# A two-layer encoder trunk in fp32 on one core: the weight sums of the MLP's second product move from VectorE to adding transfers, two products change places, and the first chunk's orders of VectorE and ScalarE are rewritten

## The reference

```python
def sqrelu_mlp(h, w_up, w_down):
    return jnp.square(jax.nn.relu(h @ w_up)) @ w_down
...
h = rmsnorm(x, g_ffn_pre[i])
x = x + rmsnorm(sqrelu_mlp(h, mlp_w_up[i], mlp_w_down[i]), g_ffn_post[i])
```

## Time and profile before

| | us |
|---|---|
| median of three runs | 1180.52 |
| the profiled execution, its own time | 1182.78 |
| its span | 1180.8 |
| TensorE busy with matmuls | 1130.0 (96% of the span) |
| VectorE busy | 946.8 (80%) |
| ScalarE busy | 766.8 (65%) |
| mean granted TensorE clock | 0.985 of full speed |

### The profile page before, as it was taken

How to read it: one execution, slowest core, us unless ns; L and a number is a source line. 1 busy time by engine, 2 the same in 40 slices (tenths; PEclk the granted TensorE clock), 3 DMA queues, 4 the chain that set the end, 5 groups by cost and what they waited for, 6 DMA issues and landing times.

```text
span 1180.8 us, 18252 instructions
## 1 busy us (share of the span) xinstructions
PE 1130.0 (96%) x6462; PEld 984.0 (83%) x6462; DVE 946.8 (80%) x1356; ACT 766.8 (65%) x1266; POOL 280.5 (24%) x261
## 2 busy tenths in 40 slices
PE   8999999997999999999999999999988999999997
PEld 7788789885897997988887888879866997988976
DVE  5899965779788688788789888875779787787787
ACT  6778867555674483674787777765547573663763
POOL 5688850302002002001421111100301011011013
PEclk9999999998999999999999999999999999999999
DMA  5322133326749549465213332223619458466653
GB/s 164 101 63 71 36 110 100 142 81 121 193 117 195 143 125 214 102 184 108 55 54 89 77 84 62 80 81 90 232 54 186 135 147 193 121 147 161 159 153 98
DMA packets 135092, 142.54 MB, mean 121 GB/s; under 512 B 5821, under 2 KB 108221, under 8 KB 134506
## 3 DMA queue, kind: packets, MB, share of 16 engines
q1 hardware_dynamic: 112300, 109.68, 29.6%
q0 software_dynamic: 22640, 31.72, 17.1%
q10 hardware_dynamic: 78, 0.16, 0.0%
HBM read 132.90 MB, written 6.29 MB: 118 GB/s over the span
## 4 chain that ended last, share of the span: by engine, by line
PE 75%; DVE 15%; issue 5%; ACT 4%; DVEq 0%; DMA 0%; POOL 0%; ACTq 0%
PE psum L860 7%; PE psum L862 7%; PE psum L861 7%; PE psum L1190 6%; PE psum L1192 6%; PE psum L1191 6%; PE psum L1178 6%; PE psum L1177 6%; PE psum L1176 6%; DVE mraw L2501 2%; DVE wlo L2157 2%; PE psum L867 2%; PE psum L869 2%; PE psum L868 2%; PE psum L1402 2%
## 5 line engine op out<-in xcount | busy, mean ns | idle before, releaser
L1495 ACT ACTIVATE whi<-mraw 128x1024 fp32r<-128x1024 f32 x212 | 223.3, 1056 | 216.6 <-PE psum L1192 85.1
L2157 DVE TENSOR_TENSOR wlo<-mraw,whi 128x1024 fp32r<-128x1024 f32 x212 | 258.5, 1223 | 101.1 <-ACT whi L1495 100.9
L1190 PE MATMUL psum<-whi,aop_hi 128*128 128x512 f32 x448 | 182.4, 407 | 29.5 <-DVE wlo L2157 14.5
L1192 PE MATMUL psum<-whi,aop_lo 128*128 128x512 f32 x448 | 179.4, 400 | 0.0
L1191 PE MATMUL psum<-wlo,aop_hi 128*128 128x512 f32 x448 | 179.2, 400 | 0.0
L860 PE MATMUL psum<-hhi,whi 128*128 128x512 f32 x376 | 150.8, 401 | 0.8 <-DVE wlo L2146 0.5
L862 PE MATMUL psum<-hhi,wlo 128*128 128x512 f32 x376 | 146.9, 391 | 0.0
L861 PE MATMUL psum<-hlo,whi 128*128 128x512 f32 x376 | 146.8, 390 | 0.0
L1190 PEld LDWEIGHTS psum<-whi,aop_hi 128*128 128x128 f32 x448 | 87.1, 195 | 56.4 <-DVE acc L2619 14.4
L1178 PE MATMUL psum<-hhi,wlo 128*128 128x256 f32 x384 | 108.7, 283 | 0.0
L1177 PE MATMUL psum<-xlo,whi 128*128 128x256 f32 x384 | 108.7, 283 | 0.0
(11 more groups left out here) (314 smaller groups left out, 2780.3 us busy)
## 6 DMA issues: line engine op xcount, KB each, us to landing
mraw<-in_mlp_w_up SPq DMA_DIRECT2D x64, 512.0 KB, 5.2
mraw<-in_mlp_w_down SPq DMA_DIRECT2D x64, 512.0 KB, 4.6
mraw<-in_mlp_w_down POOLq DMA_DIRECT2D x32, 512.0 KB, 6.1
mraw<-in_mlp_w_up POOLq DMA_DIRECT2D x24, 512.0 KB, 6.0
wraw<-in_conv_pw_w SPq DMA_DIRECT2D x20, 512.0 KB, 4.5
wraw<-in_attn_w_in SPq DMA_DIRECT2D x16, 512.0 KB, 4.9
x_copy<-xT SPq DMA_DIRECT2D x2, 2048.0 KB, 6.4
xT<-x_copy SPq DMA_DIRECT2D x2, 2048.0 KB, 9.4
```

Source lines behind the costliest of these rows:

```text
L1190: pe.matmul(o, ah, wh, start=kt == 0 and (not kept or c == 0), stop=False)
L1192: return pe.matmul(o, al, wh, start=False, stop=kt == 3 and (not kept or c == CHUNKS - 1))
L1495: a.activation(split_unit(whi, e), raw_unit(l, c, e_), ACT.Copy).then_inc(s["m_hi"], 1)
L2157: d.tensor_tensor(split_unit(wlo, e), raw_unit(l, c, e_), split_unit(whi, e).bitcast(F32), ALU.subtract).then_inc(s["m_ready"], 1)
```

## The change

1. P5's additions (both halves, all chunks) and P6's (chunks 0 to 2) leave VectorE. `add_down` now issues them as adding transfers from HBM into B11's slot, for P5, P6 and P4 alike, each when the split of the product before it in the slot is ready. VectorE keeps P6's in the last chunk, on the loaded B22.
2. In chunks 0 to 2 TensorE's order becomes P1, P2, P5, P3, P6, P7, P4; the last chunk keeps the old one. Unit numbers go by `DOWN_AT`.
3. P7's adding transfer no longer waits for P5's sum. `block_sums` has a new order: up's P4 and down's P7 alternate by half, then P5's two, then down's P6 and the next up's P7 alternating, then P4's two.
4. The next chunk's up block B11 is loaded after unit 6 of down (P3's in the new order), where it was after unit 8. The x copy is issued ahead of the first chunk's down loads.
5. In the first chunk, unit 7's split moves: on ScalarE from behind `s_hi` of pair 0 to behind the fifth square, on VectorE from behind the fourth `relu` to behind two `h_whole`. Splits 8 to 11, `h_whole`, `s7` and the others are put in another order around it, and the two P5 additions there go.

```diff
+DOWN_ORDER = ((P1, P2, P5, P3, P6, P7, P4),) * 3 + ((P1, P2, P5, P6, P3, P7, P4),)
+DOWN_AT = tuple({i: 2 * n for n, i in enumerate(o)} for o in DOWN_ORDER)
...
@@ sync, mlp_loads
+                sp.wait_ge(s["x_done"], (KB, 3 * KB)[l])
+                sp.dma_start(x_copy, flat(xT[:, :, :])).then_inc(x_kept, 16)
                 for j, b in enumerate((B11, B21, B12, B22)):
                     for h in range(2):
                         down_half(0, b, h, 2 * j + 2)
-                    if j == 1:
-                        sp.wait_ge(s["x_done"], (KB, 3 * KB)[l])
-                        sp.dma_start(x_copy, flat(xT[:, :, :])).then_inc(x_kept, 16)
...
-                    for b, at_ in ((B12, 3), (B11, 9), (B21, 11), (B22, 13)):
+                    for b, at_ in ((B12, 3), (B11, 7), (B21, 11), (B22, 13)):
@@ gpsimd, add_down
                     pool.wait_ge(*loaded(r[B12], h, 2 * (CHUNKS * l + c) + 2))
-                    pool.wait_ge(s["t_sum"], t_nth(l, c, "down", h))
...
-                    pool.wait_ge(s["m_ready"], MLP_UNITS * l + DOWN[c] + 2 * P6 + h + 1)
-                    g.dma_start(raw_half(r[B11], h, D // 2), down_block(l, c, B21, h),
+                    last_use = {P5: P1, P6: P5, P4: P6}[i]
+                    pool.wait_ge(s["m_ready"], MLP_UNITS * l + DOWN[c] + DOWN_AT[c][last_use] + h + 1)
+                    g.dma_start(raw_half(r[B11], h, D // 2), down_block(l, c, PLUS[i], h),
                                 accum_op=ALU.add).then_inc(v4_sum[h], 16)
@@ gpsimd, block_sums
-                    for i in (P7, P4):
-                        for h in range(2):
-                            add_down(l, c, i, h)
-                        for h in range(2 if c < CHUNKS - 1 else 0):
-                            add_up(l, c + 1, i, h)
+                    for h in range(2):
+                        if c:
+                            add_up(l, c, P4, h)
+                        add_down(l, c, P7, h)
+                    for h in range(2):
+                        add_down(l, c, P5, h)
+                    for h in range(2 if c < CHUNKS - 1 else 0):
+                        add_down(l, c, P6, h)
+                        add_up(l, c + 1, P7, h)
+                    for h in range(2):
+                        add_down(l, c, P4, h)
@@ scalar, first chunk (the whole list of up)
                 for i in range(4):
                     up_square(g, 2 * i)
+                    if i == 2:
+                        m_hi(l, 7)
                     if i < 3:
                         up_square(g, 2 * i + 1)
                     else:
-                        m_hi(l, 10)
+                        m_hi(l, 8)
+                        m_hi(l, 9)
                     a1_hi(g, i)
                     if i == 3:
+                        m_hi(l, 10)
                         up_square(g, 7)
                     a2_hi(g, i)
                     if i == 3:
                         m_hi(l, 11)
                     s_hi(g, i)
-                    if i < 3:
-                        m_hi(l, i + 7)
@@ vector, first_up: the new order
+ relu 0, relu 1, m_lo 6, s7 0, s_sums 0, a1_lo 0, a_lo 0
+ relu 2, s_lo 0, relu 3, s7 1, s_sums 1, a1_lo 1, a_lo 1
+ relu 4, s_lo 1, h_whole 0-1, m_lo 7, relu 5, s7 2, s_sums 2, a1_lo 2, a_lo 2
+ relu 6, s_lo 2, h_whole 2-4, m_lo 8, s7 3, m_lo 9, a1_lo 3, h_whole 5-7
+ m_lo 10, relu 7, s_sums 3, a_lo 3, m_lo 11, s_lo 3, h_sum S5
@@ vector, up_chunk
-                add_block(l, c, P5, 0)
...
-                add_block(l, c, P5, 1)
@@ vector, down_chunk
-                add_block(l, c, P6, 0)
                 add_product(g, P1)
                 m_lo(l, n + 5)
-                add_block(l, c, P6, 1)
                 m_lo(l, n + 6)
                 add_product(g, P2)
...
                 add_product(g, P5)
                 m_lo(l, n + 10)
+                m_lo(l, n + 11)
+                m_lo(l, n + 12)
                 add_product(g, P6)
@@ vector, last_down_chunk
-                add_block(l, c, P6, 0)
                 add_product(g, P1)
                 m_lo(l, n + 5)
-                add_block(l, c, P6, 1)
+                add_block(l, 0)
+                add_product(g, P2)
                 m_lo(l, n + 6)
-                add_product(g, P2)
+                add_block(l, 1)
                 m_lo(l, n + 7)
```

More of the change, by code:

```diff
@@ L90, in t_nth, with v4_nth @@
 def t_nth(l, c, phase, k):
-    return 28 * l + (8 * c - 4 if c else 0) + (4 if c and phase == "down" else 0) + k + 1
+    return 14 * l + (4 * c - 4 if phase == "up" else 12) + k + 1
+def v4_nth(l, c, phase, i):
+    return 14 * l + 4 * c + (0 if phase == "up" else {P5: 1, P6: 2, P4: 3 if c < CHUNKS - 1 else 2}[i])
 def v_nth(l, c, phase):
@@ L431, in raw_unit @@
         else:
-            i, h = divmod(e - UP_OF[c], 2)
+            n, h = divmod(e - UP_OF[c], 2)
+            i = DOWN_ORDER[c][n]
             r = down_slots(l, c)[BLOCK[i]]
@@ L1285, in mlp @@
                             up_product(l, c, h, i)
-                    for i in range(7):
+                    for i in DOWN_ORDER[c]:
                         last = c == CHUNKS - 1 and i in ((P4,), (P7, P4))[l]
@@ L1485, in m_hi @@
                 else:
-                    i, h = divmod(e_ - UP_OF[c], 2)
+                    n, h = divmod(e_ - UP_OF[c], 2)
+                    i = DOWN_ORDER[c][n]
                     if i == P7:
                         act.wait_ge(v7_sum[h], 16 * v7_nth(l, c, "down", h))
[L1489 to L1492, removed]
+                    elif i == P6 and c == CHUNKS - 1:
+                        act.wait_ge(s["t_sum"], t_nth(l, c, "down", h))
+                    elif i in (P5, P6, P4):
+                        act.wait_ge(v4_sum[h], 16 * v4_nth(l, c, "down", i))
                     else:
@@ L1887, in mlp @@
                     s_hi(g, i)
-                    if i < 3:
-                        m_hi(l, i + 7)
                 n = DOWN[0]
[L1891 to L1895, removed]
+                for j, (kept_, forms) in enumerate(((P1, (A11, S7)), (P2, (A12,)), (P5, (S2,)), (None, (S5, A22)),
+                                                    (P6, (S4,)))):
+                    m_hi(l, n + 4 + 2 * j)
+                    m_hi(l, n + 5 + 2 * j)
+                    if kept_ is not None:
+                        keep_product(l, kept_)
                     for form in forms:
@@ L2623, in first_up @@
                 g = CHUNKS * l
[L2624 to L2648, removed]
+                relu(g, 0)
@@ new lines, in first_up @@
+                relu(g, 1)
+                m_lo(l, 6)
+                s7(g, 0)
+                s_sums(g, 0)
+                a1_lo(g, 0)
+                a_lo(g, 0)
+                relu(g, 2)
+                s_lo(g, 0)
+                relu(g, 3)
+                s7(g, 1)
+                s_sums(g, 1)
+                a1_lo(g, 1)
+                a_lo(g, 1)
+                relu(g, 4)
+                s_lo(g, 1)
+                for k in range(2):
+                    h_whole(l, k)
+                m_lo(l, 7)
@@ new lines, in first_up @@
+                relu(g, 5)
+                s7(g, 2)
+                s_sums(g, 2)
+                a1_lo(g, 2)
+                a_lo(g, 2)
+                relu(g, 6)
+                s_lo(g, 2)
+                for k in range(2, 5):
+                    h_whole(l, k)
+                m_lo(l, 8)
+                s7(g, 3)
+                m_lo(l, 9)
+                a1_lo(g, 3)
+                for k in range(5, KB):
+                    h_whole(l, k)
+                m_lo(l, 10)
+                relu(g, 7)
@@ L2649, in first_up @@
+                s_sums(g, 3)
+                a_lo(g, 3)
+                m_lo(l, 11)
+                s_lo(g, 3)
                 h_sum(l, S5)
-                h_sum(l, S7)
-                m_lo(l, 12)
             def first_down(l):
                 n = DOWN[0]
-                add_block(l, 0, P6, 0)
+                m_lo(l, n + 4)
+                h_sum(l, S7)
                 m_lo(l, n + 5)
                 h_sum(l, S2)
-                add_block(l, 0, P6, 1)
                 m_lo(l, n + 6)
@@ L2660, in first_down @@
                 h_sum(l, S4)
+                m_lo(l, n + 7)
                 form_rest(l, A11)
[L2662 removed]
+                m_lo(l, n + 8)
                 form_rest(l, S7)
[L2664 removed]
+                m_lo(l, n + 9)
                 form_rest(l, A12)
[L2666 removed]
+                m_lo(l, n + 10)
                 form_rest(l, S2)
[L2668 removed]
                 m_lo(l, n + 11)
                 form_rest(l, S5)
+                m_lo(l, n + 12)
@@ L2729, in down_chunk @@
                 m_lo(l, n + 10)
+                m_lo(l, n + 11)
+                m_lo(l, n + 12)
                 add_product(g, P6)
-                for e in range(11, 15):
-                    m_lo(l, n + e)
+                m_lo(l, n + 13)
+                m_lo(l, n + 14)
                 add_up_block(l, c + 1, P6, 0)
```

27 lines of the change are left out of this document (11 added, 16 removed).

## The result

| | before | changed |
|---|---|---|
| median of four runs, us | 1179.78 | 1195.36 |
| lowest, highest | 1179.04, 1180.78 | 1193.63, 1197.98 |
| ratio to before, 95% interval | | 1.0133 (1.011 to 1.0157) |
| profiled execution, span | 1182.78, 1180.8 | 1194.17, 1192.4 |

The forecast was 1146 us, in a range of 1139 to 1160. The sign was wrong.

The account below looks back on a forecast made before the run. TensorE was taken as the bound, busy 1130.0 of 1180.8 us. Gains of 18.7 + 17.0 - 1.7 = 34.0 us from 1182.8 leave 1148.8; the median is 2.3 lower, so 1146 us, range 1139 to 1160.

Parts of the forecast that it names:

- The stops of 1.98 us: Later chunks' down parts, P5 waiting for P1's addition: all six go, with four slow stretches, 18.7 us.
- The first chunk: First down chunk: long stop of 4.18 us goes, small stops stay; gain 8.6 us in layer 0, 8.4 in layer 1.
- The slow stretch: TensorE at 1.2 GHz behind a stop, half lost; 3.45 us regained behind the long stop in each layer.
- The queue: Later chunks' down parts: six adding transfers in a row at 3.45 us each, all in time for TensorE, cost 0.
- margins of 1.6 and 2.1 us, and no stop: Down parts of chunks 1 and 2: P6's and P4's second halves land that far ahead of TensorE's need.
- the whole gain of 28.4 in stops: TensorE's stops in the down parts of both layers: 8.4 + 8.1 + 11.9 = 28.4 us.
- Without the cover ScalarE's whole list would stop there: Later chunks, P5's half: its transfer lands before ScalarE takes it, which covers the added wait; nothing waits.
- Next late would be the splits behind it: Later chunks, behind P1's addition: splits run at one per 2.7 us and now have VectorE time to spare.
- C: Rival, chance 0.05: chained sums overrun the queue, P6 and P4 stop TensorE in six chunks; 1185 to 1190 us.
- one window's 11.9%: Plain loads' share beside the down part's adding transfers between 362 and 381 us, cited against the fuller-queue rival, chance 0.13.

Follow-up runs that it names:

- up's P7 a quarter: The changed kernel, but the adding transfers for up's P7 move only a quarter of their data, the rest of those sums left out; 1151.6 us, ratio 0.975.
- copies first: The changed kernel, but in up's chunks ScalarE takes two copies out of PSUM before unit 5's split, not behind it; 1174.2 us, ratio 0.993.
- both mends: The changed kernel with up's P7 half 1 issued behind P4's transfers and ScalarE's two copies ahead of unit 5's split; 1159.7 us, ratio 0.984.
- P5 with sums later: P5 only, with three `h_whole` and the block sums of h moved behind later splits in the first chunk; 1164.1 us, ratio 0.986.
- loads wait: The changed kernel, but SyncE's down loads wait in each later chunk until up's first P4 transfer has landed; 1166.3 us, ratio 0.989.
- P5 only: The changed kernel, but P6's additions are back on VectorE and P6 before P3 on TensorE; 1150.7 us, 1147.7 in a second trial.

## Why the prediction was wrong

- **The stops of 1.98 us: right.** Counted from the part's start, the addition begins 0.2 us sooner than was worked out; all six went, with their four slow stretches.
- **The first chunk: right** in size. 4.18 and its slow stretch gone; 2.3 and 1.9 us of small stops left where 3.2 was forecast. The slow stretch was counted too high: it began 1.3 us before the long stop ended in layer 0 and 0.7 in layer 1, so the two gave 5.9 us and not 6.9.
- **The queue: nearly right in rate, and asked the wrong question.** A transfer took 3.45 us in the sum. By the span of their packets the six in a row took 20.6 us in chunk 0, 3.4 each, and 22.7 and 22.2 in chunks 1 and 2, 3.8 and 3.7 (21.6, 22.7 and 22.2 in layer 1). In chunk 1 P4's second half was there at 387.4, 2.3 us later than the 385.1 of the sum, and still in time for TensorE. P5's transfers, said to land in 5.8 to 8.7 us, took 7.4 to 12.5 in the later chunks; ScalarE waited for them 2.8 us at most, and TensorE not at all. In four of the experiments (up's P7 a quarter, copies first, both mends, and P5 with sums later) they took up to 16.9 us in the last chunk of layer 1, and one stop of 1.5 to 2.5 us at P5 followed.
- **The step that failed** is in the part on the queue. I checked each landing against the moment at which TensorE wants the unit ("margins of 1.6 and 2.1 us, and no stop") and put the cost at 0. But before the change ScalarE had begun the split of P4's second half 8.0 us ahead of that unit's first matmul; now it began 3.3 ahead (2.7 in chunk 0 of layer 1), and the 4.7 us between were not spare: they are the lead with which the splits enter the up part. There a chain with a transfer of its own (P6's split, transfer, P4's split, within three units of 2.9 us) lives on it. In place of 0 the six up parts behind these down parts stopped for 32.0 us, more than the whole gain of 28.4 in stops. "Without the cover ScalarE's whole list would stop there" was said of P5's wait and not asked of P4's, whose followers in ScalarE's order are the next up part's first splits.
- **It ended the account too early.** "Next late would be the splits behind it" was looked for in the down part only. The sum went from chunk to chunk as if each part started from rest.
- **Two things made a small lateness large.** ScalarE keeps TensorE's copies behind the split that waits (copies first: -21 us), and catching up sets off plain loads that slow the transfer it waits for (loads wait: -29 us). Neither was among the rivals. C named the link of the sums to each other and the queue, with stops at P6's and P4's own halves, and 1185 to 1190 us at 5 us for a transfer. The time came out on its side, not by its mechanism: no such stop is in the trace in chunks 1 and 2, and a transfer took at most 3.8.
- By the Trainium skill (DMA: Bandwidth & Descriptors, Queues, rings and completion order) an engine goes round its queues packet by packet. The loads-wait run agrees: with down's loads held, the first halves took 5.9 to 7.2 us in place of 9.3 to 10.3. I had used the rule for the down part alone, and weighed it by one window's 11.9%.

What stays open: why the slow clock came with all six up stops and only with four of the six short ones before; in the other traces, too, stops of about 2 us have it sometimes. And why a load 0.9 us behind the transfer slows it and one 1.9 us behind doesn't: the loads were held or not, but their distance was never set on its own.

## What to carry to other kernels

When a feed (here the splits of weights) runs ahead of the engine it feeds, an edit that uses up the lead costs nothing where it is made and is paid where the next wait of the same feed is. So check a moved operation twice: against the time at which its own user wants it, and against the time at which it was done before, and follow the difference through the in-order list of the engine that waits, past the end of the stage, until a place where it is made good. What else stands in that list behind the wait, and what the catching up will set off at once, belongs to the price.

## What the runs showed of the hardware that was not expected

- An adding transfer of 512 KB that lands in 6.0 us alone takes 8.7 to 10.5 when a plain load is issued 0.9 us behind it (in the changed kernel a second follows at 2.0); issued 1.9 us ahead of the first load it keeps its 6.0.
- Six adding transfers in a row span 20.6 to 22.7 us, 3.4 to 3.8 each, with 76% of the 16 engines in 362 to 387 us. The median from issue to landing of all down sums is 9.0 us, the most 13.0; before, P4's alone had 6.1 and 8.7.
- The lower clock came with each of the six up stops of the changed kernel, and in all traces kept with every stop of 3.0 us or more in the MLP; of those of about 2 us only some had it. It can begin while TensorE still stands. In P5 only, whose largest stop in the MLP is 1.3 us, the mean granted clock is 0.998 against 0.985 before.
